# All products of the high weights of a panel before those of the low weights, on one core of a Trainium2 chip

## The reference

```
h = x + mixer(rms_norm(x))                    # products with w_in and w_out
h = h + experts(rms_norm(h))                  # scores; 16 of 16384 experts for each of 8 heads and token
x = rms_norm(h)
x = x + 0.5 * (silu(x @ gate) * (x @ up)) @ down     # D_FF = 2816; four times in all
x = x + mlstm(x @ a_w_in) @ a_w_out           # once
k, v = rms_norm(x) @ w_kv                     # once
x = x + dilated_attention(x @ b_w_q, k, v) @ b_w_out   # once
```

## Time and profile before

| | |
|---|---|
| time, median of 3 runs | 4292.24 us (4284.7 to 4296.47) |
| the profiled execution's own time | 4296.63 us |
| its span, first to last instruction | 4294.8 us |
| mean granted TensorE clock | 0.933 of full speed |
| PE busy | 3777.9 us, 88% |
| DVE, POOL, ACT busy | 2245.2, 1952.1, 1503.3 us |

### The profile page before, as it was taken

The page is one execution under the profiler, slowest core; times in us unless marked ns, Lnnn a source line. Parts: engine busy times, 40 slices in busy tenths (PEclk is TensorE's granted clock), DMA queues, the critical chain, the costliest instruction groups (busy, mean ns, idle before and its releaser), DMA issues. The chain is left out here.

```text
span 4294.8 us, 51143 instructions
## 1 busy us (share of the span) xinstructions
PE 3777.9 (88%) x17668; PEld 3146.6 (73%) x17668; DVE 2245.2 (52%) x3388; ACT 1503.3 (35%) x2617; POOL 1952.1 (45%) x1517
## 2 busy tenths in 40 slices
PE   6948998997888889999989884999979998469999
PEld 5526888997888889988867722788758886247887
DVE  4662696884899976663326225433243321544330
ACT  3222444663222233354322312343234422233432
POOL 3724565335666667755533300444435543004444
PEclk9978999998999999999999966999989999579999
DMA  3002344457999979733332200232313335002322
GB/s 117 15 25 83 113 157 139 147 196 283 344 334 337 338 283 352 283 98 98 93 122 62 78 0 0 85 96 91 91 59 98 97 94 106 33 1 85 97 90 91
DMA packets 172780, 570.20 MB, mean 133 GB/s; under 512 B 15457, under 2 KB 58593, under 8 KB 155140
## 3 DMA queue, kind: packets, MB, share of 16 engines
q1 hardware_dynamic: 152244, 427.68, 30.6%
q0 software_dynamic: 20432, 141.31, 9.0%
HBM read 518.85 MB, written 50.07 MB: 132 GB/s over the span
## 5 line engine op out<-in xcount | busy, mean ns | idle before, releaser
L262 POOL TENSOR_TENSOR weight_low<-weight_ring,weight_high 128x512 fp32r<-128x512 f32 x1264 | 1720.1, 1372 | 1906.1 <-ACT weight_high L234 1032.8
L277 PE MATMUL banks<-normed_high,weight_high 128*128 128x512 f32 (+1 forms) x2592 | 973.1, 375 | 118.4 <-POOL weight_low L262 115.3
L278 PE MATMUL banks<-normed_low,weight_high 128*128 128x512 f32 (+1 forms) x2592 | 962.8, 371 | 0.0
L279 PE MATMUL banks<-normed_high,weight_low 128*128 128x512 f32 (+1 forms) x2592 | 962.1, 371 | 0.0
L277 PEld LDWEIGHTS banks<-normed_high,weight_high 128*128 128x128 f32 x2592 | 494.2, 191 | 203.5 <-POOL weight_low L262 136.9
L236 ACT ACTIVATE weight_high<-weight_ring 128x512 fp32r<-128x512 f32 (+1 forms) x632 | 389.6, 616 | 673.9 <-PE banks L279 673.9
L234 ACT ACTIVATE weight_high<-weight_ring 128x512 fp32r<-128x512 f32 x632 | 398.5, 631 | 612.6 <-PE banks L279 511.4
L278 PEld LDWEIGHTS banks<-normed_low,weight_high 128*128 128x128 f32 x2592 | 494.3, 191 | 62.9 <-issue 0.5
L279 PEld LDWEIGHTS banks<-normed_high,weight_low 128*128 128x128 f32 x2592 | 493.4, 190 | 62.7
L277 PE MATMUL banks<-parked_high,weight_high 128*128 128x384 f32 x768 | 271.4, 353 | 58.6 <-POOL weight_low L262 32.3
L1733 DVE TENSOR_TENSOR square<-square,banks 128x512 f32<-128x512 f32 x88 | 60.6, 688 | 416.7 <-PE banks L279 415.9
(11 more groups left out here) (364 smaller groups left out, 6022.9 us busy)
## 6 DMA issues: line engine op xcount, KB each, us to landing
weight_ring<-in_experts SPq DMA_DIRECT2D x256, 512.0 KB
weight_ring<-in_ffn_gate SPq DMA_DIRECT2D x88, 512.0 KB
weight_ring<-in_ffn_up SPq DMA_DIRECT2D x88, 512.0 KB
weight_ring<-in_ffn_down SPq DMA_DIRECT2D x64, 512.0 KB
expert_gates<-spread_space SPq DMA_DIRECT2D x6, 4096.0 KB, 12.2
parked_space<-expert_gates SPq DMA_DIRECT2D x24, 768.0 KB
parked_space<-parked_activations SPq DMA_DIRECT2D x24, 768.0 KB
weight_ring<-in_a_w_in SPq DMA_DIRECT2D x28, 512.0 KB
```

Of the source, the lines that this page charges most:

```text
L262: m.nc.gpsimd.tensor_tensor(m.w_lo[:, s % PARTS, at], m.ring[:, s, at], m.w_hi[:, s % PARTS, at].bitcast(FP), ALU.subtract).then_inc(done, 1)
L277: m.nc.tensor.matmul(out, w_hi, hi(c), start=(first and c == 0), stop=False)
L278: m.nc.tensor.matmul(out, w_hi, lo(c), start=False, stop=False)
L279: ins = m.nc.tensor.matmul(out, w_lo, hi(c), start=False, stop=(last and c == chunks - 1))
```

## The change

In `part_products` the loop over the chunks becomes two. The first does the two products with the high weights for all chunks, and waits for ACT's first and second high half. The second does the product with the low weights for all chunks, and waits for POOL's halves. `ready`, the check for gated inputs, goes with the first loop. The release of the first half goes with the second. The counts of the high semaphores start at 0, those of the low ones at 4, which `high_count` takes off.

```diff
+def high_count(at):
+
+    return at - SLOTS
+
@@ def part_products(m, pe, at, out, s, chunks, hi, lo, first, last, ready=None):
     half = HALF // P
+    pe.wait_ge(m.half_high, high_count(at))
+    for c in range(chunks):
+        if c == half:
+            pe.wait_ge(m.high, high_count(at))
+        if ready:
+            ready(c)
+        w_hi = m.w_hi[:, s % PARTS, c * P:(c + 1) * P]
+        m.nc.tensor.matmul(out, w_hi, hi(c), start=(first and c == 0), stop=False)
+        m.nc.tensor.matmul(out, w_hi, lo(c), start=False, stop=False)
     pe.wait_ge(m.half_low, at)
     for c in range(chunks):
         if c == half:
             pe.wait_ge(m.low, at)
-        if ready:
-            ready(c)
-        w_hi = m.w_hi[:, s % PARTS, c * P:(c + 1) * P]
         w_lo = m.w_lo[:, s % PARTS, c * P:(c + 1) * P]
-        m.nc.tensor.matmul(out, w_hi, hi(c), start=(first and c == 0), stop=False)
-        m.nc.tensor.matmul(out, w_hi, lo(c), start=False, stop=False)
         ins = m.nc.tensor.matmul(out, w_lo, hi(c), start=False, stop=(last and c == chunks - 1))
         if c == half - 1:
             ins.then_inc(m.half_used, 1)
```

## The result

The change made the kernel faster: 4202.92 us (4196.13 to 4204.51) against 4294.35 (4284.7 to 4301.25) for the kernel before on the same chip, a ratio of 0.978 with a 95% interval of 0.977 to 0.979. That is 91 us, three times the 30.5 that were forecast, and outside the range. The profiled execution of the changed kernel took 4202.15 us.

A forecast was written before the change was run, and what follows sets the result against it. TensorE, busy 3777.9 of 4294.8 us, was taken as the bound, so its standing still counted. Terms 10.4 + 13 + 3.5 - 1.2 + 3.5 + 1.3 = 30.5 us took the median from 4292.2 to 4262 us, range 4245 to 4285.

The forecast's parts named there:

- parked panels: Parked stage: VectorE's work makes TensorE's waits slack; gates asked for earlier cost the last group 1.2 us (-1.2).
- rival B: Parked stage: low halves hit one more VectorE operation a panel, 80 panels lose up to 77 us, 4338; chance 0.07.
- The cost of the release: Both weight buffers: first half given back 8 matmuls (1.4 us) later; cost 0, or 0.6 us without cover.
- Block starts: Eight blocks: TensorE starts with Pool, not after its subtraction; 1.3 us each, 10.4 in all.
- Route: The route's 56 gate panels: most waits under 1.3 us go; gain 13 us, between 1.4 and 17.
- Late panels: 994 to 1070 us: three more waits, 4.7 us together, shrink; gain 3.5 us (0 to 4.7).
- Experts: Expert groups: starts win 1.5 us twice, six small waits 2.5, gates cost 2; sum +3.5 us (0 to 6.6).
- first feed-forward: First feed-forward: one wait of 1.29 us goes whole; gain 1.3 us.
- Gates: Expert groups' first panels: eighth gate asked for earlier, panel ends 0.9 us later in three groups; taken as -2.
- Rival A: Only the starts win; Pool's bursts and transfers pace route, late panels and experts: 9.9 us, 4282; chance 0.15.
- Rival C: Whole kernel: route and expert gains lost at transfers, block starts ended by other waits: 0 to 5 us, 4290; chance 0.08.

The follow-up runs named there:

- the run with narrow low halves: Kernel before, but Pool subtracts only 64 of 512 columns of each low half in the 96 parked output panels: 4218.57 us, ratio 0.983.
- the same order by halves: Against the kernel before: high, then low products of the first four chunks, then of the last four; release kept at matmul 12: 4266.34 us, ratio 0.994.
- the run at 4370 us: Kernel before, with ScalarE's two small operations on a gathered row one panel later in its queue in the parked stage: 4370.04 us, ratio 1.018.
- by halves with late release: The kernel by halves that took 4266, with the first half released at matmul 20 instead of 12: 4203.11 us, ratio 0.978.
- 4232 and 4293 us: Kernel before, only the first half's release moved to matmul 20 of 24: four executions from 4232.2 to 4251.8 us, six from 4292.1 to 4302.0.
- 4236 and 4374: Order of before, release at matmul 20, ScalarE's gathered-row operations one panel later: 4236.4, 4239.8 and 4242.4 us, and twice 4374.

## Why the prediction was wrong

**The step that failed** is in the parked panels: "VectorE works 462 of 492 us, so TensorE's waits are slack". The 462 were read as work. Some 120 of them were VectorE standing at Pool's low halves: its product, cast and subtraction are busy 251 us in the stage before, and 130 in the run with narrow low halves, where none of them is lengthened. The change took away 70 of the 120: the same 582 instructions take 392.1 us after. Both numbers that would have shown it were in hand: the subtraction at 1.52 and at 0.56 us in one stage. They were used for the loss alone (rival B: one more collision a panel, up to 77 us), and never for the gain that lies in losing one. B's sign was wrong, and its size, near the 66 us won, was luck: it counted 80 subtractions at 0.96 us. These are the same operations over the whole parked stage, before and then after:

```profile
L1294 DVE TENSOR_TENSOR parked_low<-parked_space,parked_high 128x384 fp32r<-128x384 f32 x88 | 111.8, 1270 | 3.0
...
L1292 DVE CAST parked_high<-parked_space 128x384 fp32r<-128x384 f32 x88 | 91.0, 1035 | 3.0
```

```profile
L1303 DVE TENSOR_TENSOR parked_low<-parked_space,parked_high 128x384 fp32r<-128x384 f32 x88 | 54.0, 613 | 3.1
...
L1301 DVE CAST parked_high<-parked_space 128x384 fp32r<-128x384 f32 x88 | 38.1, 433 | 3.0
```

Before, 65 of the 88 subtractions were long already (62 us over 0.56 each), and 22 of the 88 casts (59 us over 0.36), which B didn't count at all: it spoke of instructions with two SBUF inputs and priced the subtraction, and the cast has one input. Only one panel of the 88 had neither. Nearly every panel had its collision already. After, 47 panels have one, most of them at the product, which became 41 us longer. The sentence brought against B, "Pool's phase there is set by VectorE", was true, and it was the very thing that the change undid.

**The cost of the release** was the second miss. "The first half of both weight buffers is given back 8 matmuls later, 1.4 us" was priced by what it could delay: "0, but 0.6 us if that cover were gone". Its effect was on what ScalarE waits for: TensorE (86 panels) in place of VectorE. The late release alone, in the same order by halves, brought 63 us, where the prediction had 0; nothing else in the change is worth as much.

**What was right.** The rest of the kernel: forecast 30.5 + 1.2 = 31.7 us without the parked term, measured 28 with the new order everywhere but in that stage.

- Block starts, 1.3 each: TensorE's idle before them fell from 17.71 to 16.60, 18.00 to 16.58, 2.40 to 1.28. The mixer's first start won 1.7 and the lead was down to 0.6 at its second block, so one of the eight was partly lost; why was not tested.
- Route, 13 us, evacuations over some 239 us: counted as in the prediction, from 472.39 to the last evacuation at 708.95, it is now 236.6 against 251.7. 15.1 us won, inside the bounds of 1.4 to 17. Giving the high weights back still earlier added nothing.
- Late panels, 3.5: the lead grows only from 18.2 to 18.7 across them. The wait at the stage's start is gone (1.40 us), but the 4.7 us of other waits, all for Pool, became 2.7 for ScalarE and 1.8 for Pool: in one of them the high half itself is late now, which the new order can't hide. Over-sized by 3.
- Experts, 3.5, and first feed-forward, 1.3: the lead grew by 3.45 and 1.35 across them. In the experts this is partly luck, for the gates cost twice what was taken off for them.
- Gates: "the panel ends at 5.1 instead of 4.2" was 5.33, 5.37 and 5.18 in three groups, and the run that asks for them later took most of it away. Right there; but the first group, put at nothing, went from 4.31 to 5.72. Before, the four took 4.31, 4.70, 4.33 and 4.22, so all cost 4.0 us and not 2.
- Rival A (DMA or Pool's bursts pace the parked stage): the DMA share rose from 0.91 to 0.99 with the quicker panels and held nothing back. Rival C (0 to 5 us in all) falls too: the rest of the kernel alone won 28.

**The mechanism.** Rival B named a rule of the Trainium skill; a second page of it bears on the rows of the run at 4370 us, where VectorE's product took 5.18 us beside Pool's 5.03. The Trainium skill (SBUF — State Buffer, section "SBUF: two separate sides") says that the port pair shared by VectorE and GpSimd is an exclusive lock, held for a whole instruction, and that the loser doesn't slow down but stands. The trace agrees that VectorE stands. The usual subtraction of 1.52 fits a wait for one instruction: the one at 1294.03 in the kernel before ends 0.41 us after the first low half of the pair, which ended at 1295.15. The other rows go further: the product stood through four Pool instructions, and the cast of 3.07, which began 0.3 us ahead of the pair, through both. No run here shows what decides whether VectorE gets in between two of them.

**What stays open.** Why in the old order the release at matmul 20 leads to the quick pattern in some executions and not in others, where the kernels that start at the high half and hold Pool back were quick in all of theirs (the changed kernel, by halves with late release, and four more, four executions each). It was argued, not shown, that in the old order TensorE starts at Pool's first low half, so that its release follows Pool and closes the ring again. Also open is the start of the parked stage, where the changed kernel too begins in the slow pattern: groups of 47.5 and 41.1 us, 44.1 and 33.8 without collisions, so some 11 us are left there. None of the kernels tried beats the changed one by more than can be measured.

## What to carry to other kernels

An engine's busy time can contain another engine's: when one operation has two durations in one stage, price the stage at the shorter one before calling it the bound, and price the loss and the gain of the collision alike. Where engines release each other in a ring, ask of every wait which engine it makes the next one follow, for a later release or an added wait can be a gain (63 us here) by tying a helper to the engine that should set the pace. And run a kernel several times when such a ring exists: one program gave 4232 and 4293 us, another 4236 and 4374.

## What the runs showed of the hardware

VectorE's operations of 128x384 with inputs and output in SBUF (the memory that holds tiles and weights; PSUM is where TensorE writes its sums) have sharply different durations beside Pool's 128x512 subtractions: the subtraction 0.56 alone and 1.52 beside a pair, the product 0.55 and 1.61 to 1.67, and 5.18 beside four back to back. The cast, which has one input, 0.36 and 3.07. Beside Pool's 128x64 subtractions of 0.42 us none of them is lengthened, though most overlap one. VectorE's dot products and row additions, whose second input is in PSUM, kept their 1.21 and 1.28 us in all kernels. Pool pays less: its pair of low halves took 2.89 us in the slow pattern and 2.55 in the quick one.
